# A hybrid encoder with a mixture of experts: the last four experts' rows combined on chip, three of them before the last gate and up

## The reference

```python
h = rms_norm(x, norm2_g[l])
x = x + hier_moe(h, ...)

def hier_moe(h, w_rg, b_rg, w_re, b_re, w_gate, w_up, w_down):
    ...   # each token: best of 4 groups, then the best 2 of its 8 experts, with weights gate
    def expert_block(args):
        rows, e = args
        xb = x_pad[rows]
        return (jax.nn.silu(xb @ w_gate[e]) * (xb @ w_up[e])) @ w_down[e]
    ys = ys.reshape(n_rows, D) * buf_w[:, None]
    out = jax.ops.segment_sum(ys, buf_tok, num_segments=T + 1)[:T]
```

## Time and profile before

| | us |
|---|---|
| median of 3 runs | 1663.07 (1662.14 to 1663.87) |
| the profiled execution's own time | 1666.44 |
| its span | 1664.3 |
| TensorE matmuls busy | 1556.2 (94% of the span) |
| VectorE busy | 629.5 (38%) |
| ScalarE busy | 430.9 (26%) |
| GpSimd busy | 374.5 (23%) |
| mean granted clock of TensorE | 0.982 |

### The profile page before, as it was taken

The page is one execution under the profiler, slowest core; times in us unless marked ns, Lnnn a source line. Parts: engine busy times, 40 slices in busy tenths (PEclk is TensorE's granted clock), DMA queues, the critical chain, the costliest instruction groups (busy, mean ns, idle before and its releaser), DMA issues.

```text
span 1664.3 us, 20438 instructions
## 1 busy us (share of the span) xinstructions
PE 1556.2 (94%) x8292; PEld 821.3 (49%) x8292; DVE 629.5 (38%) x1226; ACT 430.9 (26%) x778; POOL 374.5 (23%) x440
## 2 busy tenths in 40 slices
PE   8999999979999999998799999998999999999975
PEld 4655666546444444443356546655554444444422
DVE  1686635471221222211417856364512211222115
ACT  3554740211111111111235647303111111111112
POOL 5472860000000000000364539400000000000003
PEclk9999999989999999999999999999899999999998
DMA  9200303659999999999930012065699999999996
GB/s 395 118 1 13 140 1 86 272 208 401 412 427 427 428 426 426 427 427 427 362 151 1 1 41 113 1 196 234 250 371 421 426 427 426 427 428 426 429 428 245
DMA packets 54082, 468.77 MB, mean 282 GB/s; under 512 B 18985, under 2 KB 19113, under 8 KB 27458
## 3 DMA queue, kind: packets, MB, share of 16 engines
q1 hardware_dynamic: 46738, 451.12, 65.6%
q0 software_dynamic: 7104, 16.24, 2.7%
q10 hardware_dynamic: 144, 0.07, 0.0%
HBM read 446.44 MB, written 26.74 MB: 284 GB/s over the span
## 4 chain that ended last, share of the span: by engine, by line
PE 73%; DMA 18%; DVE 5%; ACT 2%; issue 1%; POOL 0%; SPq 0%; POOLq 0%; DVEq 0%
PE bank L884 20%; DMA ring<-wu 18%; PE bank L551 11%; PE bank L914 9%; PE bank L687 7%; PE bank L876 6%; PE bank L860 2%; PE bank L626 2%; PE bank L545 2%; PE bank L613 2%; PE bank L641 2%; PE bank L522 1%; PE bank L901 1%; PE bank L741 1%; PE bank L539 1%
## 5 line engine op out<-in xcount | busy, mean ns | idle before, releaser
L884 PE MATMUL bank<-ring,hbuf 128*64 128x512 f32 x704 | 312.8, 598 | 21.8 <-DMA ring<-wu 21.8
L885 PE MATMUL bank<-ring,hbuf 128*64 128x512 f32 x704 | 313.2, 599 | 0.0
L2046 POOL DMA_INDIRECT expert_rows<-raw_qd,store_rows x60 | 58.8, 980 | 1066.1 <-ACT raw_qd L1276 894.9
L1799 DVE COPY raw_qd<-bank 128x256 f32<-128x256 f32 x64 | 27.2, 425 | 699.4 <-PE bank L901 696.7
L551 PE MATMUL bank<-hbuf,ring 128*128 128x512 f32 x480 | 210.0, 594 | 0.0
L884 PEld LDWEIGHTS bank<-ring,hbuf 128*64 128x64 f32 x704 | 95.8, 138 | 220.9 <-issue 220.8
L914 PE MATMUL bank<-ring,raw_qd 128*64 128x512 f32 x352 | 160.5, 598 | 5.2 <-DVE raw_qd L1799 4.1
L884 PE MATMUL bank<-raw_qd,hbuf 128*64 128x512 f32 x320 | 145.9, 610 | 16.2 <-DMA hbuf<-wu 13.9
L916 PE MATMUL bank<-ring,raw_qd 128*64 128x512 f32 x352 | 160.5, 598 | 0.0
L876 PE MATMUL bank<-raw_qd,x 128*128 128x192 f32 x896 | 159.5, 332 | 0.0
L1269 ACT ACTIVATE raw_qd<-bank 64x512 f32<-64x512 f32 x64 | 37.8, 590 | 445.7 <-PE bank L885 445.7
(11 more groups left out here) (374 smaller groups left out, 2251.0 us busy)
## 6 DMA issues: line engine op xcount, KB each, us to landing
ring<-wg SPq DMA_DIRECT2D x44, 2048.0 KB, 22.9
ring<-wu SPq DMA_DIRECT2D x44, 2048.0 KB, 27.7
ring<-wd SPq DMA_DIRECT2D x44, 2048.0 KB, 26.6
ninth_slot<-wd SPq DMA_DIRECT2D x20, 2048.0 KB, 27.6
hbuf<-wu SPq DMA_DIRECT2D x20, 2048.0 KB, 27.6
raw_qd<-wg SPq DMA_DIRECT2D x20, 2048.0 KB, 22.9
ring<-w_in SPq DMA_DIRECT2D x8, 2048.0 KB, 14.2
ring<-w_out SPq DMA_DIRECT2D x4, 2048.0 KB, 8.5
```

The lines of the kernel that those rows point to most:

```text
L884: mm(pb[2 + par][0:CAP, :], tokens[:, k, :], gates[:, k, :], start=(k == 0), stop=(k == KT - 1))
L885: last = mm(pb[2 + par][CAP:P, :], tokens[:, k, :], ups[:, k, :], start=(k == 0), stop=(k == KT - 1))
L2046: G.indirect_dma_start(out=half_rows, out_offset=bass.IndirectOffsetOnAxis(ap=store_i[:, e:e + 1], axis=0), in_=y_sb[e % 2], in_offset=Non ...
```

## The change

Rows of experts 28 to 31 are no longer stored; LATE, the number of stored experts, goes from 30 to 28. Their weight matrices are turned at experts 22, 24, 26 and 28. Experts 28 and 29 are combined behind the transposes of hidden rows of 30 (batch 0), expert 30 behind its down (batch 1), expert 31 at the end (batch 2). Gate and up of 31 move from ahead of the transposes of 30 to behind batch 1, on TensorE and ScalarE. The first two batches use four banks (0, 1, 6, 7) in turn, so each block waits for the add that frees its banks. VectorE does the adds of batches 0 and 1 and all eight operations of gathered rows between the transposes' copy of expert 30 and hidden rows of 31. The gathers wait for the fourth turned matrix and for gate and up of 29. In SyncE's queue down of 30 goes ahead of gate and up of 31.

```diff
-LATE = NE - 2
+LATE = NE - 4
...
-        GATHERED, COMPLETE = (1, 3, 6, 9), (5, 8, 11, 12)
-        WEIGHED, COUNTED = (22, 24), 27
+        ADDED = 5 * NB
+        COMPLETE = range(ADDED - NB + 1, ADDED + 1)
+        WEIGHED, COUNTED = (22, 24, 26, 28), 27
+        FIRST_OVER = len(WEIGHED) + 3 * NB
+        EARLY_BANK = (0, 6, 0, 6)
...
             for e in range(3, NE):
                 at = 3 * (e % 3)
+                if e == NE - 1:
+                    down_weights(e - 1)
                 sp.wait_ge(s["gu"], e - 2)
...
-                if e >= 4:
+                if 4 <= e < NE - 1:
                     down_weights(e - 1)
...
             for e in range(NE):
-                if e + 1 < NE:
+                if e + 1 < NE - 1:
                     gate_up(e + 1)
                 hidden(e)
+                if e == NE - 2:
+                    pe.wait_ge(s["cv"], 2 * len(WEIGHED))
+                    pe.wait_ge(s["ye"], e)
+                    for b in range(NB):
+                        if b >= 2:
+                            pe.wait_ge(s["moe"], on("moe") + b - 1)
+                        combined(b, list(zip(selT[0:2], y_sb)), EARLY_BANK[b])
...
+                if e == NE - 2:
+                    pe.wait_ge(s["ye"], e + 1)
+                    for b in range(NB):
+                        pe.wait_ge(s["moe"], on("moe") + NB + b - 1)
+                        combined(b, [(selT[2], y_sb[0])], EARLY_BANK[b])
+                    gate_up(NE - 1)
...
-            pe.wait_ge(s["cv"], 4)
             pe.wait_ge(s["ye"], NE)
             for b in range(NB):
-                combined(b, list(zip(selT, y_sb)))
+                combined(b, [(selT[3], y_sb[1])], 2 * b)
...
             hidden_rows(0)
             for e in range(NE):
                 hidden_t(e)
+                if e == NE - 2:
+                    dve.wait_ge(s["kept"], on("kept") + NB)
+                    for batch in range(2):
+                        for b in range(NB):
+                            combined(b, batch)
+                    for b in range(NB):
+                        gathered_rows(b)
                 if e + 1 < NE:
                     hidden_rows(e + 1)
...
-            dve.wait_ge(s["kept"], on("kept") + NB)
-            gathered_rows(0)
-            gathered_rows(1)
-            combined(0)
-            gathered_rows(2)
-            combined(1)
-            gathered_rows(3)
-            combined(2)
-            combined(3)
+            for b in range(NB):
+                combined(b, 2)
...
-            pool.wait_ge(s["cb"], 2)
-            pool.wait_ge(s["gu"], LATE)
+            pool.wait_ge(s["cb"], len(WEIGHED))
+            pool.wait_ge(s["gu"], NE - 2)
```

More of the change, by code:

```diff
@@ L223, in trunk @@
         gathered = [raw[:, 0:1024], raw[:, 8192:9216], raw[:, 1024:2048], raw[:, 2048:3072],
-                    qd[:, 0:1024], qd[:, 1024:2048], hbuf[:, 4096:5120], hbuf[:, 5120:6144]]
+                    qd[:, 0:1024], qd[:, 1024:2048], hbuf[:, 4096:5120], raw[:, 7168:8192]]
         weighted, weighted_t = (raw[:, 2048 + 512 * i:2560 + 512 * i].rearrange("p (b s) -> p b s", b=NB) for i in range(2))
-        selT = [tile(raw, at) for at in (3584, 4608)]
+        selT = [tile(raw, 3584), tile(raw, 4608), tile(hbuf, 7680), tile(hbuf, 5632)]
         rel_late = small[:, 8:16]
@@ L495, in sync_program @@
                 sp.wait_ge(s["dn"], all_done)
-                sp.wait_ge(s["moe"], on("moe") + 3 * NB)
+                sp.wait_ge(s["moe"], on("moe") + ADDED)
                 load_w_in(sp, layer + 1, 4)
@@ L924, in down @@
                     pe.wait_ge(s["ye"], e - 1)
+                if e == NE - 1:
+                    pe.wait_ge(s["moe"], on("moe") + 2 * NB)
                 pe.wait_ge(slot[i], loaded(i, e, layer))
@@ L932, in weights_turned, with combined @@
                 last.then_inc(s["cb"], 1)
-            def combined(b, terms):
+            def combined(b, terms, first_bank):
                 for i, (weights_, rows_) in enumerate(terms):
@@ L937, in combined @@
                         r = slice(CAP * half, CAP * half + CAP)
-                        last = mm(pb[2 * b + half][:, :], weights_[r, P * b:P * b + P], rows_[r, :],
+                        last = mm(pb[first_bank + half][:, :], weights_[r, P * b:P * b + P], rows_[r, :],
                                   start=(i == 0), stop=(i == len(terms) - 1))
@@ L990, in tensor_program @@
                     down_of(1, W_down[1])
-                    pe.wait_ge(s["cv"], pe.snap(i * 2 + 5))
+                    pe.wait_ge(s["cv"], pe.snap(i * 2 + 2 * len(WEIGHED) + 1))
                     for b in range(NB):
@@ L1273, in rows @@
                 act.wait_ge(s["dn"], e + 1)
-                if e >= 2:
+                if 2 <= e < LATE + 2:
                     act.wait_ge(y_out[par], 16 * (e // 2) + STORED * layer)
+                elif e >= LATE + 2:
+                    act.wait_ge(s["cb"], len(WEIGHED) + NB)
                 A(y_sb[par], pb[5 + par][:, :], ACT.Copy, scale=0.5).then_inc(s["ye"], 1)
@@ L1292, in scalar_program @@
                     picked(3)
+                if e == NE - 2:
+                    gate_exp(NE - 1)
                 if e == KEPT_AT:
@@ L1629, in vector_program @@
             cap = rt[10][:, 0:NE]
-            for i in range(GC // CAP):
+            for i in range(GRP):
                 TS(slot_ids[:, CAP * i:CAP * i + CAP], cst("slot_id"), float(CAP * i), None, ALU.add)
@@ L1821, in gathered_rows @@
                 for j in range(2):
-                    if j:
-                        dve.wait_ge(s["moe"], on("moe") + GATHERED[b])
+                    dve.wait_ge(s["moe"], on("moe") + (2 * NB + 2 * b + 1 if j else NB + b + 1))
                     i = NB * j + b
@@ L1826, in gathered_rows, with add_block, combined @@
                         op0=ALU.mult, op1=ALU.add).then_inc(s["moe"], 1)
-                dve.wait_ge(s["moe"], on("moe") + GATHERED[b] + 1)
-            def add_block(b):
+            def add_block(b, first_bank):
                 return TT(x[:, b, :].rearrange("p (o d) -> p o d", o=2), x[:, b, :].rearrange("p (o d) -> p o d", o=2),
-                          banks[:, 2 * b:2 * b + 2, :], ALU.add)
-            def combined(b):
-                dve.wait_ge(s["cb"], b + 3)
-                add_block(b).then_inc(s["moe"], 1)
+                          banks[:, first_bank:first_bank + 2, :], ALU.add)
+            def combined(b, batch):
+                dve.wait_ge(s["cb"], len(WEIGHED) + NB * batch + b + 1)
+                if batch:
+                    dve.wait_ge(s["moe"], on("moe") + (b + 1 if batch == 1 else 2 * NB + 2 * b + 2))
+                add_block(b, 2 * b if batch == 2 else EARLY_BANK[b]).then_inc(s["moe"], 1)
             hidden_rows(0)
@@ L1845, in vector_program @@
                     weigh_late(0)
-                if e == WEIGHED[0] + 1:
-                    weights_evacuated(0)
-                    weigh_late(1)
-                if e == WEIGHED[1] + 1:
-                    weights_evacuated(1)
+                if e - 1 in WEIGHED:
+                    weights_evacuated(WEIGHED.index(e - 1))
+                    if e + 1 in WEIGHED:
+                        weigh_late(WEIGHED.index(e + 1))
                 if e == COUNTED:
@@ L1882, in vector_program @@
                     V.tensor_copy(flat(hidT[1]), pb[4][:, 0:FT * CAP]).then_inc(s["ht_e"], 1)
-                    dve.wait_ge(s["cb"], dve.snap(i * 5 + 7))
+                    dve.wait_ge(s["cb"], dve.snap(i * 5 + FIRST_OVER + 1))
                     V.tensor_copy(selT[0], pb[7][:, :]).then_inc(s["cv"], 1)
-                    dve.wait_ge(s["cb"], dve.snap(i * 5 + 11))
+                    dve.wait_ge(s["cb"], dve.snap(i * 5 + FIRST_OVER + 5))
                     for b in range(NB):
-                        ins = add_block(b)
+                        ins = add_block(b, 2 * b)
                     ins.then_inc(s["oc"], 2)
```

15 lines of the change are left out of this document (8 added, 7 removed).

## The result

| | before | after |
|---|---|---|
| median of the runs, us | 1662.9 (1662.14 to 1663.87, 4 runs) | 1686.09 (1685.28 to 1688.85, 4 runs) |
| ratio | | 1.0137, 95% interval 1.0121 to 1.0154 |
| profiled execution, us | 1666.44 | 1686.14 |
| its span, us | 1664.3 | 1684.0 |
| mean granted TensorE clock | 0.982 | 0.981 |

The change costs 23 us by the medians and 19.7 us by the two profiled executions. The traces explain the 19.7; the rest is that the profiled execution of before lay 3.5 us above its median and that of after on it. Times of runs are medians of fast runs; one run of experiment 4, 1708.09 us at a granted clock of 0.936, was in a slower state and is left out.

The account below looks back on a forecast made before the run. Up-weight transfers were the chain's largest piece beside matmuls, with DMA engines full until the weights are in. Layer 1's +10.3 and layer 0's +11.1 us gave 21.4 on the median 1663.07: 1684.5 us, range 1673 to 1698.

Parts of the forecast that it names:

- First add at the end of the copies: VectorE's first add waits until ScalarE's four copies of x are made, 1620.66 + 4.25 = 1624.9 in layer 1.
- Batch 0, down of 30, batch 1: TensorE waits for VectorE's adds in batch 0, delaying down of 30; batch 1's adds end at 1640.5.
- Gathered rows in one stretch ahead of the hidden rows: On VectorE all eight gathered operations precede hidden rows of 31: 10.45 us, to 1651.0.
- Gate and up of 31 covered: Gate/up and tanh of 31 end at 1649.7 at most, before VectorE at 1651.0; 1.3 us of slack.
- The end: Hidden rows of 31 to last add: 12.65 us, plus 1.7 us lost to the TensorE clock, to 1665.4.
- Terms taken as nothing: Two more turned selections, two fewer stores a layer and 0.5 MB less of zeroed rows were taken to change nothing.
- GpSimd term: Final norm behind layer 1's last add: GpSimd slowed beside VectorE's adds; taken as 0, with 1 us as bound.
- Rival (a): Gathers win over the weight loads, so down weights of 29 come late: 8.6 us more a layer, 1702; chance 0.10.
- (b): Faster: everything hides in the wait for the last up weights; 4.7 us sooner, twice, 1654; chance 0.03.
- (c): No effect: needs VectorE at hidden rows of 31 within 1.6 us of 1642.4; chance 0.03.
- Rival (d): TensorE's clock stays up and its new waits cost less: 1677; within the forecast's own range, no separate chance.

Follow-up runs that it names:

- experiment 4: The changed kernel with ScalarE's four copies of x made behind the tanh of 30, ahead of the evacuation of down of 29; 1681.72 us, ratio 1.0104 to before.
- Experiment 2: The changed kernel with gathered rows spread: block 0 behind batch 0, block 1 behind batch 1, blocks 2 and 3 behind the transposes' copy of 31; 1674.77 us.
- Experiment 11: The changed kernel with six filling matmuls of unused result behind gate and up of 31; 1682.24 us, ratio 1.0102 to before.
- experiment 3: The changed kernel with the gathers held until gate and up of 30 are done, one expert later; 1687.32 us, ratio 1.0136 to before.
- Number 8: Against the changed kernel: only expert 29 combined early, old load order, copies of x early, gathered rows behind the transposes' copy of 31; 1660.31 us, ratio 0.9982 to before.

## Why the prediction was right

The forecast was 1684.5 us and the median is 1686.09; it was right in sign, in size and in mechanism. That it is within 2 us is in part luck. Its sum, 21.4, was worked out from one profiled execution and laid on the median; the profiled executions differ by 19.7 and the medians by 23.2. And inside the sum two errors offset each other: layer 0 was 2.3 too high, layer 1 0.6 too low.

- **First add at the end of the copies.** Held: 1635.34 against 1635.30. Experiment 4 takes this wait away, and hidden rows of 31 come 1.9 us sooner in each layer.
- **Batch 0, down of 30, batch 1.** The forecast had the eighth add 15.6 us behind the copies; it is 15.3. TensorE's wait for VectorE is there (1.61).
- **Gathered rows in one stretch ahead of the hidden rows.** Forecast 10.45, measured 10.15. Experiment 2 moves them, and the hidden rows start 3.7 us sooner in each layer.
- **Gate and up of 31 covered.** The side was right, the slack mis-sized: 3.7 us and not 1.3. I had put the weights at the latest possible time; the up weights of 31, issued at 1598.92, landed 42.1 us later, 8 us before TensorE was free for them. And I had taken gate and up with the 8.71 us of the earlier trace rows, which hold a stretch at the lower clock; behind batch 1, with no wait for weights ahead, they take 7.13 us to the start of the tanh (1649.24 to 1656.37).
- **The end.** Hidden rows to last add: forecast 14.35, measured 14.09. In it, down of 31 lost 1.3 us to the clock where 1.7 stood. Experiment 11 shows that this term is real and due to the idle time.
- **Terms taken as nothing.** Selections, stores and zeroed rows show no cost: layer 0 reaches its copies 0.6 us sooner than before. The GpSimd term of 0 (bound 1) held, with 9.2 us behind the last add in both kernels. End of layer 1 in the profile after:

```profile
1672.66 0.25 POOL L1027 TENSOR_SCALAR small<-small 128x1 f32<-128x1 f32 x1 [46.93 <-ACT hbuf L1021]
1672.99 0.57 POOL L1029 TENSOR_TENSOR small<-small 128x1 f32<-128x1 f32 x1
...
1676.13 1.46 POOL L1029 TENSOR_TENSOR small<-small 128x1 f32<-128x1 f32 x1
```

  The first stands beside adds that read one input from PSUM and takes 0.57; the other stands beside VectorE's L2125, with inputs in SBUF, and takes 1.46. The Trainium skill (GPSIMD Engine Reference, Specifications) lays contention between the two engines to instructions in a two-port mode or with two SBUF inputs; these rows agree with it.
- **Mis-sized.** The sum took +11.1 for layer 0, where 0.6 were gained ahead of the copies and 0.7 in the transposes of x: 8.8 reached the next layer. It took +10.3 for layer 1, where 9.3 stand behind the copies, and had no term for its last experts, +1.6. That is mostly gate and up of 30 at the lower clock (1.7 us), which experiment 2 does not have. What the early gathers do to the wait ahead of them stays open: it was 1.65 and 1.64 us in the two layers before, 1.09 and 2.01 after, and 2.78 and 1.21 with the gathers issued later (experiment 3).
- **Rival (a), gathers first.** Refuted: under load the gathers landed after 25.8 us in the median, so they did not pass the loads, and down of 29 did not wait for its weights. (Its price, 11.9 less 3 us, is 8.9 and not 8.6 a layer; that moves 1702 by less than 1.) The Trainium skill (DMA: Bandwidth & Descriptors, Queues, rings and completion order) has each DMA engine go round its queues a packet at a time; the long landing shows that the loads kept moving, but how the two sides shared the engines no row here separates.
- **Rivals (b) and (c).** They needed hidden rows within 21.7 us of the start of the copies (1642.4); they came at 29.6, behind the operations in front of them. Number 8 is what (b) needs: fewer operations ahead of them, and a combination early enough to use the wait for weights. It starts them at 1632.21.
- **Rival (d).** Experiment 11 is its first half, the clock: 1682.24, where the 3.4 us priced for it lead from the measured 1686.09 to 1682.7. Its second half, cheaper waits, was not tested together with it.

## What to carry to other kernels

Work that is moved ahead into "idle" time of an engine is free only if it ends before that engine's next link of the critical chain is due; compare the engine's sum of operations from the earliest possible start with the time at which that link is wanted, and put late work behind the link. Combine early only what is ready when TensorE waits for weights. Where a chain leaves TensorE idle ahead of its last matmuls, price the lower clock as well, and don't expect two mends to add: each moves the idle time and with it the stretch at the lower clock.
